# Up projections of two feed-forward blocks: one 512-column matmul for the high weights in place of two of 256 columns

## The reference, cut to what matters

```python
x = x + conv_ffn(rms_norm(x, ffn_norm[l]), ffn_w_up[l], ffn_conv_w[l], ffn_conv_b[l], ffn_w_down[l])   # layer 1
gt, up = jnp.split(rms_norm_2(x, g_ffn) @ w_gate_up, 2, axis=-1)                                       # layer 2
return x + (jax.nn.silu(gt) * up) @ w_down
```

## Time and profile before

| | us |
|---|---|
| median of three runs | 3180.6 (3180.09 to 3180.75) |
| the profiled execution | 3176.7 |
| its span, first to last instruction | 3174.9 |
| PE busy | 3120.3 (98%) |
| DVE busy | 1718.6 (54%) |
| ACT busy | 1155.6 (36%) |
| POOL busy | 181.0 (6%) |
| HBM traffic | 167 GB/s over the span |

### The profile page before, as it was taken

One profiled execution on the slowest core, in us unless ns is written; L12 is line 12 of the kernel. 1 busy time (PEld: TensorE's weight loads), 2 busy tenths in 40 slices (PEclk: granted clock), 3 DMA queues, 4 the chain that ended last, 5 costly groups with the idle time before them and its releaser, 6 DMA issues.

```text
span 3174.9 us, 54633 instructions
## 1 busy us (share of the span) xinstructions
PE 3120.3 (98%) x22968; PEld 2949.8 (93%) x22968; DVE 1718.6 (54%) x2148; ACT 1155.6 (36%) x1173; POOL 181.0 (6%) x80
## 2 busy tenths in 40 slices
PE   8999999999999999999999999999999999999999
PEld 8898898889999999999999977778999999999999
DVE  6663352966677777775556333312566555555443
ACT  5453102113444444344443322344444444433333
POOL 0000000000001111000000210000000111110000
PEclk9999999999999999999999999999999999999999
DMA  6553332444455555545555543223455555554555
GB/s 226 186 185 139 106 120 100 169 151 174 163 180 186 186 186 187 185 169 187 183 196 178 185 169 107 93 86 114 172 177 182 186 185 186 186 186 169 189 183 181
DMA packets 80149, 530.05 MB, mean 167 GB/s; under 512 B 9152, under 2 KB 9664, under 8 KB 27712
## 3 DMA queue, kind: packets, MB, share of 16 engines
q1 hardware_dynamic: 80064, 528.84, 47.3%
HBM read 526.71 MB, written 2.10 MB: 167 GB/s over the span
## 4 chain that ended last, share of the span: by engine, by line
PE 91%; DVE 5%; ACT 3%; issue 0%; DMA 0%; SPq 0%; ACTq 0%; DVEq 0%
PE bank L485 91%; DVE w_low L1429 2%; ACT w_high L1010 2%; DVE arena L1429 2%; ACT out_high L1034 0%; DVE out_low L1429 0%; ACT arena L1400 0%; PE bank L938 0%; DMA xT<-in_xT 0%; DVE arena L1459 0%; DVE xrs L1459 0%; ACT arena L1093 0%; DVE xtmp L1429 0%; ACT mix_high L1112 0%; DVE arena L1426 0%
## 5 line engine op out<-in xcount | busy, mean ns | idle before, releaser
L1429 DVE TENSOR_TENSOR w_low<-ring,w_high 128x2048 fp32r<-128x2048 f32 (+1 forms) x440 | 922.9, 2098 | 492.2 <-ACT w_high L1010 486.7
L1010 ACT ACTIVATE w_high<-ring 128x2048 fp32r<-128x2048 f32 (+1 forms) x448 | 788.0, 1760 | 842.9 <-DMA ring<-in_w_up 434.4
L485 PE MATMUL bank<-up_high,w_high 128*128 128x256 f32 x2816 | 791.5, 281 | 1.3 <-issue 0.8
L485 PE MATMUL bank<-h_low,w_high 128*128 128x256 f32 x2816 | 788.9, 280 | 0.0
L485 PE MATMUL bank<-up_high,w_low 128*128 128x256 f32 x2816 | 788.1, 280 | 0.0
L485 PE MATMUL bank<-hT,ring 128*128 128x256 f32 x2560 | 568.8, 382 | 0.0
L485 PEld LDWEIGHTS bank<-hT,ring 128*128 128x128 f32 x2560 | 486.9, 191 | 75.0 <-issue 9.3
L485 PEld LDWEIGHTS bank<-up_high,w_high 128*128 128x128 f32 x2816 | 530.5, 188 | 1.7 <-issue 0.9
L485 PEld LDWEIGHTS bank<-h_low,w_high 128*128 128x128 f32 x2816 | 530.7, 188 | 0.1
L485 PEld LDWEIGHTS bank<-up_high,w_low 128*128 128x128 f32 x2816 | 529.7, 188 | 0.0
L485 PE MATMUL bank<-acts_high,w_low 128*128 128x256 f32 x1408 | 397.1, 282 | 0.0
(11 more groups left out here) (272 smaller groups left out, 3935.6 us busy)
## 6 DMA issues: line engine op xcount, KB each, us to landing
ring<-in_w_up SPq DMA_DIRECT2D x176, 1024.0 KB, 4.8
ring<-in_w_down SPq DMA_DIRECT2D x128, 704.0 KB, 4.0
ring<-in_w_in SPq DMA_DIRECT2D x66, 1024.0 KB, 4.8
ring<-in_w_mix SPq DMA_DIRECT2D x62, 1024.0 KB, 4.8
ring<-in_w_gates SPq DMA_DIRECT2D x48, 1024.0 KB, 4.8
ring<-in_w_branch SPq DMA_DIRECT2D x16, 1024.0 KB, 4.8
ring<-in_w_out SPq DMA_DIRECT2D x16, 1024.0 KB, 4.8
ring<-in_w_o SPq DMA_DIRECT2D x16, 1024.0 KB, 4.8
```

Of the source, the lines that this page charges most:

```text
L485: return nc.tensor.matmul(o, lhsT, rhs, start=first, stop=last)
L1010: A(w_high[:, s, 0:cols], ring[:, s, 0:cols], ACT.Copy).then_inc(rounded[s], 1)
L1429: return V.tensor_tensor(o, a, b, op)
```

## The change

In both up projections the two matmuls that share the high weights become one of 512 columns: high and low activations of a tile are laid side by side (`up_early`, `up_late`, each [8 tiles, 2, 256]), and the product goes to both halves of the bank: half 0 gets the high activations' product, half 1 that of the low ones. The matmul of the low weights is still 256 columns into half 0. So a unit is 16 matmuls of 512 columns and 16 of 256, with 32 weight loads instead of 48. ScalarE copies half 1 of the bank to `xms` (one buffer of 256 columns; before the copy it waits until the bank of the unit before is drained) and raises `half_copied`; VectorE waits for it, adds `xms` to half 0 (this raises `drained`), and multiplies the sum by `xrs` in one more operation. In layer 2 the Silu now waits for that operation (`conv_made`), as in layer 1. In the first round ScalarE waits for `norm_done` before the first copy, since `xms` is in use until then; the rounding of unit 3 stands behind that wait.

```diff
-        h_low = alias("h_low", hT_base, [P, KT, T])
-        up_high = alias("up_high", arena_base, [P, KT, T], 78)
+        up_early, up_late = alias("up_early", hT_base, [P, 8, 2, T]), alias("up_late", arena_base, [P, 8, 2, T], 78)
+        ups = [part[:, k] for part in (up_early, up_late) for k in range(8)]
...
+            def project_pairs(pairs, waits=None):
+
+                def body(s):
+                    for k in range(KT):
+                        if waits:
+                            waits(k)
+                        c = slice(k * P, (k + 1) * P)
+                        mm(bank[s][:], w_high[:, s, c], pairs[k], k == 0, False)
+                        last = mm(bank[s][:, 0], w_low[:, s, c], pairs[k][:, 0], False, k == KT - 1)
+                    return last
+                return body
...
-            raw_unit(*up)
+            raw_unit(lambda waits: project_pairs(ups, waits))
             for j in range(3):
-                unit_split(project_split(*up))
-            rounds_split(21, project_split(*up))
+                unit_split(project_pairs(ups))
+            rounds_split(21, project_pairs(ups))
...
+            def copy_half():
+
+                p = (units.pos - 1) % RING
+                act.wait_ge(drained[p], units.drained[p].value())
+                s, _, _, there, _ = units.next()
+                act.wait_ge(consumed[s], there)
+                A(xms[:], bank[s][:, 1], ACT.Copy).then_inc(half_copied, 1)
+
+            def pair_round(i, cols, late, first=False):
 
                 for j in range(2):
-                    s, _, _, _, free = units.next()
                     round_weights(cols[2 * j])
                     if first and j == 0:
                         root()
+                        act.wait_ge(norm_done, norm[0])
+                    copy_half()
                     if late[j]:
                         act.wait_ge(ff_done, acts.value())
                         round_act(i * 2 + j - 1)
                     round_weights(cols[2 * j + 1])
-                    if convolved:
-                        convs.add()
-                        act.wait_ge(conv_made, convs.value())
-                    else:
-                        act.wait_ge(drained[s], free + 1)
+                    convs.add()
+                    act.wait_ge(conv_made, convs.value())
                     A(cv[:, 2 * j], cv[:, 2 * j], ACT.Silu).then_inc(silu_pair, 1)
-                    units.next()
+                    copy_half()
                     acts.add()
...
                 x = xtmp[:]
-                tt(x, bank[s][:, 0], xrs[:]).then_inc(drained[s], 1)
+                halves.add()
+                dve.wait_ge(half_copied, halves.value())
+                tt(x, bank[s][:, 0], xms[:], ADD).then_inc(drained[s], 1)
                 dve.wait_ge(drained[s], units.drained[s].value())
+                link(tt(x, x, xrs[:]))
...
             def scaled(n, half, o, s):
-                tt(o, bank[s][:, 0], xrs[:]).then_inc(drained[s], 1)
-                if half:
-                    dve.wait_ge(drained[s], units.drained[s].value())
+                halves.add()
+                dve.wait_ge(half_copied, halves.value())
+                tt(o, bank[s][:, 0], xms[:], ADD).then_inc(drained[s], 1)
+                dve.wait_ge(drained[s], units.drained[s].value())
+                made_half(tt(o, o, xrs[:]), half)
```

More of the change, by code:

```diff
@@ L581, in _, with raw_unit @@
             raws = [0]
-            def raw_unit(high, low, second=False):
+            def raw_unit(project, second=False):
                 n = raws[0]
@@ L589, in waits @@
                     pe.wait_ge(raw_lowered, KT * n + k + 1)
-                unit_split(project_split(high, low, waits))
+                unit_split(project(waits))
                 pe.wait_ge(raw_summed, (KT - 1) * raws[0])
@@ L857, in _ @@
                 pe.wait_ge(down_drained[b], 1 + KT // 2)
-            raw_unit(in2_high, in2_low, second=True)
+            raw_unit(lambda waits: project_split(in2_high, in2_low, waits), second=True)
             unit_split(project_split(in2_high, in2_low))
@@ L1058, in round_raw @@
                     act.wait_ge(drained[s], free + 1)
-                    A(up_high[:, n], xT[:, n], ACT.Copy, scale=v(gain, n)).then_inc(raw_rounded, 1)
+                    A(ups[n][:, 0], xT[:, n], ACT.Copy, scale=v(gain, n)).then_inc(raw_rounded, 1)
                     square_raw(n)
@@ L1283, in pair_round, with pair_rounds @@
                     round_weights(cols[2 * j + 1])
-                    if convolved:
-                        convs.add()
-                        act.wait_ge(conv_made, convs.value())
-                    else:
-                        act.wait_ge(drained[s], free + 1)
+                    convs.add()
+                    act.wait_ge(conv_made, convs.value())
                     A(cv[:, 2 * j], cv[:, 2 * j], ACT.Silu).then_inc(silu_pair, 1)
-                    units.next()
+                    copy_half()
                     acts.add()
-            def pair_rounds(first, n, late, convolved):
+            def pair_rounds(first, n, late):
                 with act.Fori(0, n) as i:
@@ L1297, in pair_rounds @@
                     acts.enter(i, 2)
-                    convs.enter(i, 2 if convolved else 0)
-                    pair_round(i + first, [UNIT] * RING, late, convolved)
+                    convs.enter(i, 2)
+                    pair_round(i + first, [UNIT] * RING, late)
                 units.leave(n)
@@ L1303, in pair_rounds, with feed_forward @@
                 convs.leave(n)
-            def feed_forward(convolved):
+            def feed_forward():
                 half = SPLIT_UP // 2
[L1307 to L1310, removed]
+                pair_round(0, [UNIT] * RING, (False, True), first=True)
+                pair_rounds(1, half - 1, (True, True))
+                pair_round(half, [UNIT] * RING, (True, False))
+                pair_rounds(half + 1, 20 - half, (False, False))
                 last = FF_TILES - 2
-                pair_round(21, [UNIT] * 2 + [DOWN * P] * 2, (False, False), convolved)
+                pair_round(21, [UNIT] * 2 + [DOWN * P] * 2, (False, False))
                 act.wait_ge(consumed[(units.pos - 1) % RING], units.consumed[(units.pos - 1) % RING].value())
@@ L1891, in residual_raw @@
                     if n:
-                        lower_raw(n - 1, up_high[:, n - 1], h_low[:, n - 1], v(gain, n - 1))
+                        lower_raw(n - 1, ups[n - 1][:, 0], ups[n - 1][:, 1], v(gain, n - 1))
                         sum_raw(n - 1)
@@ L1895, in residual_raw @@
                         dve.wait_ge(drained[s], free + 1)
-                lower_raw(KT - 1, up_high[:, KT - 1], h_low[:, KT - 1], v(gain, KT - 1))
+                lower_raw(KT - 1, ups[KT - 1][:, 0], ups[KT - 1][:, 1], v(gain, KT - 1))
                 sum_raw(KT - 1)
@@ L1972, in convolved, with made_half @@
                 last = stt(o[:, 2:], x[:, 0:T - 2], w(0), o[:, 2:], M, ADD)
+                made_half(last, half)
+            def made_half(last, half):
                 if half == 0:
@@ L2006, in feed_forward @@
                     pairs.enter(i, 2)
-                    convs.enter(i, 2 if made is convolved else 0)
+                    halves.enter(i, RING)
+                    convs.enter(i, 2)
                     pair_round(i + 1, [UNIT] * RING, made)
@@ L2012, in feed_forward @@
                 pairs.leave(20)
+                halves.leave(20)
                 convs.leave(20)
```

12 lines of the change are left out of this document (6 added, 6 removed).

## The result

The changed kernel takes 3156.2 us (median of four runs, 3155.5 to 3159.0) against 3180.7: 24.5 us less, ratio 0.9925, 95% interval 0.9913 to 0.9937. The forecast of 3171.3 had the sign but little more than a third of the size, and 3156.2 lies just outside the range of 3157 to 3183.

The account below looks back on a forecast made before the run. The prediction took TensorE to bound the kernel: -9.9 us from its merged matmuls, +0.1 and +0.5 at the ends of layers 1 and 2, -9.3 in all, so 3180.6 becomes 3171.3 us; range 3157 to 3183.

Parts of the forecast that it names:

- What bounds the kernel: Whole kernel: TensorE sets the pace, busy 98% of the span, so the distance between its matmul starts counts.
- TensorE's part: Up stages: the merge saves only a matmul's cost beside its columns, 3.5 ns a tile, 9.9 us over 2816 tiles.
- rows 4: Trace rows of the input projection before the change: 512-column fp32r matmuls with weight loads, 232.0 ns each.
- Layer 2's unit: Up stage of layer 2, where VectorE has time: its unit alone tests the matmul's price; 5.60 us if the forecast holds.
- rival 1: Up stages: load or issue spaces 256-column matmuls; 5.3 to 11.1 ns a tile, 3166 to 3150, put at 3160; chance 0.17.
- One of its two supports: Plain fp32 rows, 429 ns for 512 columns and 223 for 256: a merge there would save 16 ns.
- VectorE's part: Layer 1's up stage: the added operation raises its need from 20.04 to 22.3 us a round, level with TensorE; cost nothing.
- Its cover: Layer 1's up stage: VectorE's lowering is 5.7 us ahead of TensorE's need; 1.1 and some 2 us get used.
- ScalarE's part and the ends: Copies cost nothing beyond a 0.48 us later read; 0.1 us at layer 1's end, 0.5 at layer 2's.
- VectorE as the bound: Layer 1's up stage: VectorE needs 22.8 us a round or more, 3176 to 3181, say 3178; chance 0.20.
- the copy in its chain: Layer 1: VectorE waits for ScalarE's copy in each unit, need 24.3 us a round, 3207; chance 0.08.
- the pair saves nothing: Up stages: a merged pair takes as long as three 256-column matmuls or a little more, 3180 to 3185; chance 0.07.

Follow-up runs that it names:

- bare streams: Kernels without the computation, only fp32r matmul streams with weight loads, starts and widths varied; 512 columns alone took 227.3 to 233.3 ns by place.
- e,o,o: Stream-only kernel: activations start at a multiple of 128 bytes, high and low weights 64 bytes off; 340.0 ns a tile as three of 256, 346.6 merged.
- e,e,e: Stream-only kernel: activations, high and low weights all start at multiples of 128 bytes; 354.9 ns a tile as three of 256, 352.1 merged.

## Why the prediction came out as it did

**What bounds the kernel**: right. All of the gain lies in the two up stages and in TensorE's steps.

**TensorE's part**: this is the step that failed, and with it the forecast: "I take 3.5 ns, since rows 4 are of the same type, same weight loads and same clock". It measured 8.7. The 512-column matmuls took 227.9 and 230.3 ns instead of the 232.0 of the earlier trace rows, and the 256-column ones behind them 114.2 and 117.0 instead of 117.8. The comparison took it that columns, type, load and clock set the step. The starts of the operands in SBUF set it too, and so does what stands around the matmul: the same merge saved 8.7 ns a tile as given, 13.3 with all starts at multiples of 128 bytes, and cost 13.2 with the weights 64 bytes off. The earlier trace rows stream weights past loaded activations in tiles of three, with no matmul of 256 columns between and with their own order of starts, and bare streams of 512 columns alone took from 227.3 to 233.3 ns by the starts. "The rows of the same type" were thus not the same case. Which of these differences made their 232.0 is not shown. The trace before shows that a term is missing, if one averages: `h_low` 117.1 against `up_high` 118.5 ns, and in the 512-column stream values between 224 and 241 where a fixed cost would give one.

Layer 2's unit, by which the prediction wanted to test the price, is 5.513 us (most often), between its 5.60 and the 5.5 of rival 1. The 8.7 lies inside that rival's 5.3 to 11.1 ns: that matmuls of 256 are spaced by their load or issue gave 3160 with a chance of 0.17 and came nearest. That its number fits is in part luck. One of its two supports was a misreading: the 16 fp32 matmuls of 256 columns in the earlier trace rows were taken as 223 ns each, but in the trace one distance is 320 ns and the others are 215 or 216, so with 429 for 512 columns a merge would save 3 ns there and not 16. These rows speak for the forecast, and yet the forecast was too small for fp32r. Its cause is half right: a short load does make a 256 quicker (120.0 to 113.3 ns), but in another placement three matmuls with full loads step by 113.3 ns too, and there the merge loses. The range failed by 1 us because its lower end was put inside that rival and not at the end of its bound of 3150.

The Trainium skill ("TensorE: Matmul & The Clock Gate", section "Step-by-step: what each phase is for") says that loading the next tile's weights takes no SBUF read bandwidth from the running matmul. For fp32r matmuls of 256 columns the load is not free of effect in time all the same: 120.0 against 113.3 ns by its size alone, and 340.2 to 360.2 ns a tile by 64 bytes of placement. Whether it is the reading of SBUF that collides, against the page, no run here shows.

**VectorE's part**: right that it hides behind TensorE, too dear by 0.7 us a round. In the first rounds of the loop, while VectorE was behind, its rounds took 21.61 us where the sum said 22.3: the added operation stands 0.45 us before the next one instead of 0.57, and the 0.28 us gap is there once, as before, not a second time. That is 0.5 of the 0.7. It caught up by 0.4 us a round until it stood 0.9 us behind ScalarE's copy. Its cover was put at 4.6 less 2 and measured about 5 in all, start included.

**ScalarE's part and the ends**: right. Copy and add cost 0.5 us in all by the stages of the run without them (its time is also 0.5 lower, which is within the spread of the runs), where the sum has 0.6; TensorE's waits for lowered weights stay at 21.2 us, and those for VectorE's results in the arena go from 2.2 to 2.7 us, the 0.5 of the `drained_all` in layer 2.

**The other rivals**: VectorE as the bound and the copy in its chain did not come in. The first was near: one linked operation more brings it, at 28.6 us. That the pair saves nothing did not come in either, but it names what happens, and worse, after a shift of 64 bytes.

**Open**: why the starts count as they do. Only offsets of 0 and 64 bytes were tried, so the period is not shown. Bare streams give the kernel's value for some kinds only: e,o,o pairs 346.6 ns bare and 353.4 in the kernel, e,e,e pairs 352.1 and 346.9, e,e,e as three 354.9 and 360.2. By the bare streams the merge would gain 2.8 ns a tile with all at multiples of 128 bytes and lose 6.6 with the weights moved; in the kernel it gained 13.3 and lost 13.2. Tiles of one placement differ by position and by layer, so the order of what runs before has a part in it. The placement was tried for fp32r alone.

## What to carry to other kernels

Before a matmul's step is carried from one stage to another, check that the operands' starts in SBUF stand to each other in the same way and that the same kinds of matmul stand around it, and average the distances over hundreds of starts for each operand's name: a few ns a matmul are the whole effect here. In a kernel that TensorE bounds with 256-column fp32r matmuls, try the placement of weights against activations (0 or 64 bytes) before a rewrite, in the kernel itself: it gave 69 us for nine changed lines here, and the rewrite 24.5. And a merge should be judged in the placement that is kept, since the same edit gave -36, -24.5 and +39.5 us in three.

## What the runs showed of the hardware

- 64 unused bytes in each partition ahead of a buffer moved the whole kernel by 1.0% (3180.7 to 3213.9 us), and the merged one by 0.7% (3156.2 to 3178.1).
- The quickest fp32r steps seen at the upper clock were 113.3 ns for 256 columns and 226.7 for 512, 0.443 ns a column; 320, 384 and 448 columns took 0.458, 0.452 and 0.461.
- Tiles of three matmuls of 256 columns with both weights on the other half of 128 bytes than the streamed operand took 113.3 ns a matmul with full loads, in the bare stream and in the kernel; on the same half 120.0 in the kernel. A bare stream of one kind stepped by 117.8 on opposite halves and 119.8 to 120.0 on the same half, there 113.3 with a load of 32 columns.
- Weight transfers, ScalarE's rounding and VectorE's subtraction beside a stream of pairs changed its step by 0.2 ns or less in the arena's placement. In the hT region one stream, the one beside the transfers, took 350.0 instead of 340.5 ns a pair.
